# Stacking the high and low parts of the experts' results on the partitions of one product, in a two-layer kernel

## The reference, cut to what matters

```
expert = (g_idx * M_PER_GROUP + e_idx).reshape(-1)        # 2 of 32 experts per token
xs  = xt[tok_sorted]                                      # tokens, by expert
hid = silu(ragged_dot(xs, w_gate, sizes)) * ragged_dot(xs, w_up, sizes)   # 1024 -> 512
ys  = ragged_dot(hid, w_down, sizes) * weight             # 512 -> 1024
return segment_sum(ys, tok_sorted, num_segments=n_tok)    # back to the 512 tokens
```

## Time and profile before

| | |
|---|---|
| median of 3 runs | 2735.05 us (2734.01 to 2735.18) |
| profiled execution | 2735.55 us, its span in the trace 2733.7 us, 1.85 us around it |
| mean granted TensorE clock | 0.982 |
| PE busy | 2618.6 us (96%) |
| PEld / DVE / ACT / POOL busy | 1859.7 / 1461.6 / 749.7 / 114.4 us |
| bytes | 559.82 MB, mean 205 GB/s |
| the two expert stages, by the first and last start of their lines | about 226 to 730 and 1010 to 1515 us |

### The profile page before, as it was taken

One profiled execution on the slowest core, in us unless ns is written; L12 is line 12 of the kernel. 1 busy time (PEld: TensorE's weight loads), 2 busy tenths in 40 slices (PEclk: granted clock), 3 DMA queues, 4 the chain that ended last, 5 costly groups with the idle time before them and its releaser, 6 DMA issues. The chain is left out here.

```text
span 2733.7 us, 39425 instructions
## 1 busy us (share of the span) xinstructions
PE 2618.6 (96%) x15526; PEld 1859.7 (68%) x15526; DVE 1461.6 (53%) x2028; ACT 749.7 (27%) x1205; POOL 114.4 (4%) x238
## 2 busy tenths in 40 slices
PE   8997999999799979999999699999999999999999
PEld 7674555555476665555555577888888877888887
DVE  4755444444654554444444676656552666556632
ACT  3530000000145510000000343543332454433331
POOL 0000000000000000000000000000000010000000
PEclk9998999999899989999999899999999999999999
DMA  6249999999322089999997132223332312223331
GB/s 171 82 169 373 388 409 408 411 407 401 116 77 93 37 309 388 405 405 403 408 405 299 53 106 77 93 77 102 99 123 93 101 62 93 78 93 99 102 123 54
DMA packets 168109, 559.82 MB, mean 205 GB/s; under 512 B 17394, under 2 KB 100914, under 8 KB 118322
## 3 DMA queue, kind: packets, MB, share of 16 engines
q1 hardware_dynamic: 162546, 549.68, 53.4%
q0 software_dynamic: 5440, 8.40, 1.0%
HBM read 561.17 MB, written 6.29 MB: 208 GB/s over the span
## 5 line engine op out<-in xcount | busy, mean ns | idle before, releaser
L1401 DVE TENSOR_TENSOR resid<-resid,ps 128x1024 f32<-128x1024 f32 x252 | 306.8, 1218 | 237.7 <-PE ps L1321 237.7
L229 PE MATMUL ps<-l_h_hi,l_w_hi 128*128 128x512 f32 x896 | 352.9, 394 | 0.0
L230 PE MATMUL ps<-l_h_lo,l_w_hi 128*128 128x512 f32 x896 | 348.8, 389 | 0.0
L231 PE MATMUL ps<-l_h_hi,l_w_lo 128*128 128x512 f32 x896 | 348.7, 389 | 0.0
L1308 PE MATMUL ps<-first_weights,moe_xsT 128*64 128x256 f32 x2688 | 326.2, 384 | 0.0
L2885 DVE TENSOR_TENSOR l_w_lo<-l_raw,l_w_hi 128x2048 fp32r<-128x2048 f32 x76 | 174.0, 2292 | 270.6 <-ACT l_w_hi L2630 270.3
L1308 PEld LDWEIGHTS ps<-first_weights,moe_xsT 128*64 128x64 f32 x2688 | 191.5, 137 | 133.0 <-issue 67.4
L1373 ACT ACTIVATE moe_ys_hi<-ps 128x512 fp32r<-128x512 f32 x64 | 38.2, 597 | 687.3 <-PE ps L1347 687.3
L2630 ACT ACTIVATE l_w_hi<-l_raw 128x2048 fp32r<-128x2048 f32 x76 | 145.6, 1918 | 180.6 <-PE ps L231 161.1
L229 PEld LDWEIGHTS ps<-l_h_hi,l_w_hi 128*128 128x128 f32 x896 | 168.2, 188 | 37.6 <-issue 2.9
L230 PEld LDWEIGHTS ps<-l_h_lo,l_w_hi 128*128 128x128 f32 x896 | 168.3, 188 | 35.4 <-issue 1.4
(11 more groups left out here) (611 smaller groups left out, 4621.8 us busy)
## 6 DMA issues: line engine op xcount, KB each, us to landing
first_weights<-in_moe_w_up SPq DMA_DIRECT2D x84, 1024.0 KB, 11.5
first_weights<-in_moe_w_down SPq DMA_DIRECT2D x84, 1024.0 KB, 10.4
first_weights<-in_moe_w_gate SPq DMA_DIRECT2D x84, 1024.0 KB, 11.2
first_ring<-in_moe_w_up SPq DMA_DIRECT2D x44, 1024.0 KB, 11.7
first_ring<-in_moe_w_down SPq DMA_DIRECT2D x44, 1024.0 KB, 10.7
l_raw<-in_ffn_up SPq DMA_DIRECT2D x44, 1024.0 KB, 5.1
first_ring<-in_moe_w_gate SPq DMA_DIRECT2D x40, 1024.0 KB, 10.9
l_raw<-in_w_in SPq DMA_DIRECT2D x22, 1024.0 KB, 5.2
```

Source lines behind the costliest of these rows:

```text
L229: pe.matmul(out, stationary[0], moving[0], start=first, stop=False)
L230: pe.matmul(out, stationary[0], moving[1], start=False, stop=False)
L231: return pe.matmul(out, stationary[1], moving[0], start=False, stop=last)
L1401: dve.tensor_tensor(row, row, sums(t), ALU.add).then_inc(added, 1)
```

## The change

Four things change together, with the semaphores that go with them.

1. `ys_hi` and `ys_lo` become one tile `ys` [128, 2, 512]. For half h the 64 result rows stand twice on the partitions: high parts on the rows where the result lies, low parts on the other 64. One 128-row product per half with the same `sel` (whose 128 rows hold the slots twice) adds both. ACT and DVE write `ys` in two instructions each, one for each half of the partitions.
2. A row is gathered as two half rows: 128 indices, 128 rows of 2 KB, first halves on partitions 0-63, second halves on 64-127. `lay` makes the indices (twice the token, plus 0 or 1) for all 128 rows at once.
3. `turn_rows` transposes in pairs, one piece from each partition half, into two banks (`turned`); gate, up and the turned rows change places in PSUM.
4. The semaphores `sel_made` and `ys_low` become one, `parts_made`, with three counts per block; the wait for `ys_low` before the down products and one wait for `hid_kept` are gone; a wait for `silued` stands before `turn_rows`.

```diff
-            ins.then_inc(self.listed, 1)
+        ins.then_inc(self.listed, 1)
...
         dve.wait_ge(x.listed, 1)
-        dve.tensor_copy(x.near[0:SLOTS, :], k.ps[0:SLOTS, 3, 0:COLS]).then_inc(x.near_kept, 1)
-        dve.wait_ge(x.near_kept, 1)
-        dve.scalar_tensor_tensor(r.take[0:SLOTS, :], k.ps[0:SLOTS, 3, COLS:2 * COLS], float(NO_ROW), x.near[0:SLOTS, :], ALU.add, ALU.add).then_inc(x.done, 1)
+        link(dve.tensor_scalar(x.near[:, :], k.ps[:, 3, 0:COLS], float(NO_ROW), None, ALU.add))
+        link(dve.tensor_tensor(r.token, k.ps[:, 3, COLS:2 * COLS], x.near[:, :], ALU.add))
+        dve.tensor_scalar(r.take[:, :], r.token, 2.0, k.cst[:, C_HALF:C_HALF + 1], ALU.mult, ALU.add).then_inc(x.done, 1)
...
-    row_of_tile = xs[:, :].rearrange("s (c p j) -> s c j p", c=2, j=4)
+    row_of_tile = xs[:, :].rearrange("s (p j) -> s j p", j=4)
-    TURN, UP_BANK, DOWN, GATE = 0, 1, 2, 3
-    gate_out = lambda rows: k.ps[rows, GATE, 0:256]
+    TURN, GATE, DOWN, UP_BANK = 0, 1, 2, 3
+    gate_out = lambda rows: k.ps[rows, GATE, 256:512]
+    turned = k.ps[:, TURN:GATE + 1, 0:256]
...
-                pool.indirect_dma_start(out=xs[:, :], out_offset=None, in_=r.x_dram,
+                pool.indirect_dma_start(out=xs[:, :], out_offset=None, in_=r.half_rows,
                                         in_offset=bass.IndirectOffsetOnAxis(ap=take[:, 0:1], axis=0),
-                                        bounds_check=SEQ - 1, oob_is_err=False).then_inc(rows_in, 16)
+                                        bounds_check=2 * SEQ - 1, oob_is_err=False).then_inc(rows_in, 16)
...
-                wait_then_tick(pool, sel_made, b + 1, tick_pool)
+                wait_then_tick(pool, parts_made, 3 * b + 1, tick_pool)
...
             def turn_rows():
-                for j in range(ND):
-                    ins = pe.transpose(k.ps[:, TURN, j * SLOTS:(j + 1) * SLOTS], row_of_tile[:, j // 4, j % 4, :], k.cst[0:SLOTS, C_ID:C_ID + SLOTS])
+                for i in range(4):
+                    for c in range(2):
+                        rows_ = slice(64 * c, 64 * c + 64)
+                        ins = pe.transpose(turned[:, c, i * SLOTS:(i + 1) * SLOTS], row_of_tile[rows_, i, :], k.cst[rows_, C_ID + 64 * c:C_ID + 64 * c + 64])
...
                 if t == 0:
-                    wait_then_tick(pe, sel_made, b + 2, tick_pe)
-                    wait_then_tick(pe, ys_low, b + 2, tick_pe)
+                    wait_then_tick(pe, parts_made, 3 * b + 4, tick_pe)
...
-                for part in (ys_hi, ys_lo):
-                    for h in range(2):
-                        rows_ = slice(64 * h, 64 * h + 64)
-                        ins = pe.matmul(sums(t)[:, h, :], sel[rows_, t * P:(t + 1) * P], part[rows_, :], start=part is ys_hi, stop=part is ys_lo)
+                for h in range(2):
+                    ins = pe.matmul(sums(t)[:, h, :], sel[:, t * P:(t + 1) * P], ys[:, h, :], start=True, stop=True)
...
                 wait_then_tick(pe, xsT_kept, b + 1, tick_pe)
-
-                wait_then_tick(pe, hid_kept, b + 1, tick_pe)
...
                 wait_then_tick(pe, rows_in, b * 16 + 32, tick_pe)
+                wait_then_tick(pe, silued, b + 1, tick_pe)
                 turn_rows()
-                wait_then_tick(pe, hid_kept, b + 2, tick_pe)
+                wait_then_tick(pe, hid_kept, b + 1, tick_pe)
...
                 wait_then_tick(pe, hidT_kept, b + 1, tick_pe)
-                wait_then_tick(pe, ys_low, b + 1, tick_pe)
...
-                act.activation(ys_hi[:, :], k.ps[:, DOWN, :], ACT.Copy).then_inc(ys_kept, 1)
+                for h in range(2):
+                    rows_ = slice(64 * h, 64 * h + 64)
+                    act.activation(ys[rows_, h, :], k.ps[rows_, DOWN, :], ACT.Copy).then_inc(ys_kept, 1)
...
-                dve.tensor_scalar(sel[:, :], iota[:, :], slot[:, 1, :], None, ALU.is_equal).then_inc(sel_made, 1)
-                dve.wait_ge(ys_kept, b + 1)
-                dve.tensor_tensor(ys_lo[:, :], k.ps[:, DOWN, :], ys_hi[:, :].bitcast(F32), ALU.subtract).then_inc(ys_low, 1)
+                dve.tensor_scalar(sel[:, :], iota[:, :], slot[:, 1, :], None, ALU.is_equal).then_inc(parts_made, 1)
+                for h in range(2):
+                    high, low = slice(64 * h, 64 * h + 64), slice(64 - 64 * h, P - 64 * h)
+                    dve.wait_ge(ys_kept, 2 * b + h + 1)
+                    dve.tensor_tensor(ys[low, h, :], k.ps[high, DOWN, :], ys[high, h, :].bitcast(F32), ALU.subtract).then_inc(parts_made, 1)
```

More of the change, by code:

```diff
@@ L67 @@
 C_TOK = C_ISLOT + P
-C_MASKA = C_TOK + NT
+C_HALF = C_TOK + NT
+C_MASKA = C_HALF + 1
 C_MASKS = C_MASKA + 2 * P
@@ L107, in constants @@
     c[:, C_TOK:C_TOK + NT] = i[:, None] + P * np.arange(NT)
+    c[:, C_HALF] = i // SLOTS
     c[:, C_MASKA:C_MASKA + P] = np.where(i[None, :] > i[:, None], 0.0, NEG)
@@ L267, in __init__ @@
         self.le = plan.put("le", le_kb, [1, MORE_COLS, EXPERTS])
-        self.xs = plan.put("xs", xs_kb, [SLOTS, D])
-        self.ys_lo = plan.put("ys_lo", le_kb, [P, 512], F32R)
+        self.xs = plan.put("xs", xs_kb, [P, D // 2])
+        self.ys = plan.put("ys", le_kb - 2, [P, 2, 512], F32R)
         self.sel, self.iota = plan.put("sel", first_kb, [P, SEQ], F32R), plan.put("iota", first_kb + 2, [P, SEQ])
@@ L283, in __init__ @@
         (self.w_in, self.x_out, self.turned, taken_first, taken_second, self.made, self.shifted, self.ratioed, self.expd, self.chosen, self.ranked, self.laid,
-         self.listed, self.done, self.emptied, self.near_kept) = (st.sem(n) for n in (
-            "rw_in", "x_out", "rows_turned", "rows_taken_first", "rows_taken_second", "logits", "gshifted", "ratioed", "gexpd", "chosen", "ranked", "laid", "listed", "done", "emptied", "near_kept"))
+         self.listed, self.done, self.emptied) = (st.sem(n) for n in (
+            "rw_in", "x_out", "rows_turned", "rows_taken_first", "rows_taken_second", "logits", "gshifted", "ratioed", "gexpd", "chosen", "ranked", "laid", "listed", "done", "emptied"))
         self.taken = (taken_first, taken_second)
@@ L426, in lay @@
         ins.then_inc(x.laid, 1)
[L427 to L430, removed]
+        dve.wait_ge(x.listed, 2)
         link(dve.tensor_copy(x.near[:, :], k.ps[:, 7, 0:COLS]))
@@ L442, in first_rows @@
         pool.wait_ge(self.done, 1)
-        pool.indirect_dma_start(out=self.xs[:, :], out_offset=None, in_=r.x_dram,
-                                in_offset=bass.IndirectOffsetOnAxis(ap=r.take[0:SLOTS, 0:1], axis=0),
-                                bounds_check=SEQ - 1, oob_is_err=False).then_inc(r.rows_in, 16)
+        pool.indirect_dma_start(out=self.xs[:, :], out_offset=None, in_=r.half_rows,
+                                in_offset=bass.IndirectOffsetOnAxis(ap=r.take[:, 0:1], axis=0),
+                                bounds_check=2 * SEQ - 1, oob_is_err=False).then_inc(r.rows_in, 16)
     def list_experts(self, k, dve, link, r, listed):
@@ L1140, in __init__ @@
         self.x_dram = nc.dram_tensor(f"{name}_x", (SEQ, D), F32, kind="Internal").ap()
+        self.half_rows = self.x_dram.rearrange("s (h d) -> (s h) d", h=2)
 class ExpertWeights:
@@ L1205, in experts @@
     silu, hid, hidT = st.sb("silu", [P, 256]), st.sb("hid", [P, 256]), st.sb("hidT", [P, 2, P])
-    take, slot = st.sb("take", [SLOTS, 1], I32), st.sb("slot", [P, 2, 1])
-    ys_hi, ys_lo, sel, iota = st.sb("ys_hi", [P, 512], F32R), rt.ys_lo, rt.sel, rt.iota
-    (take_set, slot_set, rows_turned, xsT_kept, silued, hid_kept, hid_turned, hidT_kept, ys_kept, ys_low, sel_made, combined, added, tick_sp, tick_pool, tick_pe, chain,
+    take, slot = st.sb("take", [P, 1], I32), st.sb("slot", [P, 2, 1])
+    ys, sel, iota = rt.ys, rt.sel, rt.iota
+    (take_set, slot_set, rows_turned, xsT_kept, silued, hid_kept, hid_turned, hidT_kept, ys_kept, parts_made, combined, added, tick_sp, tick_pool, tick_pe, chain,
      expert_set, grown, first_hi) = (st.sem(n) for n in (
-         "take_set", "slot_set", "rows_turned", "xsT_kept", "silued", "hid_kept", "hid_turned", "hidT_kept", "ys_kept", "ys_low", "sel_made", "combined", "added",
+         "take_set", "slot_set", "rows_turned", "xsT_kept", "silued", "hid_kept", "hid_turned", "hidT_kept", "ys_kept", "parts_made", "combined", "added",
          "tick_sp", "tick_pool", "tick_pe", "chain", "expert_set", "grown", "first_hi"))
     rows_in = r.rows_in
-    row_of_tile = xs[:, :].rearrange("s (c p j) -> s c j p", c=2, j=4)
+    row_of_tile = xs[:, :].rearrange("s (p j) -> s j p", j=4)
     hid_of_tile = hid[:, :].rearrange("s (p j) -> s j p", j=2)
@@ L1254, in gather @@
             def gather(b):
-                pool.tensor_copy(take[:, :], r.take[0:SLOTS, bass.ds(b, 1)]).then_inc(take_set, 1)
+                pool.tensor_copy(take[:, :], r.take[:, bass.ds(b, 1)]).then_inc(take_set, 1)
                 wait_then_tick(pool, take_set, b, tick_pool)
-                pool.indirect_dma_start(out=xs[:, :], out_offset=None, in_=r.x_dram,
```

(9 more changed lines are left out.)

3 lines of the change are left out of this document (1 added, 2 removed).

## The result

The changed kernel took 2746.09 us (median of 5 runs, 2742.57 to 2750.44) against 2734.09 us (5 runs, 2733.82 to 2735.18) of the kernel before on the same chip: a ratio of 1.0044 [1.0031, 1.0057], 12.0 us slower. The forecast was 2744.3. The profiled execution of after is the longest of its five (2750.44 us, span 2748.6).

What follows compares the result with a forecast made beforehand. PE was taken to set the pace, with DMA keeping up. Terms 38.4 - 21.1 - 9.6 + 0 + 1.5 = +9.2 us gave 2744.3 us on the median's scale, range 2727 to 2767.

Steps and rivals of the forecast that it cites:

- A: Chain before combine t=0: ACT and DVE in 64-row halves end 0.60 us later per block, +38.4 us (34 to 44).
- B, turn in pairs: `turn_rows`: transposes in pairs let hidden transposes start 0.33 us sooner per block, until `hid` limits: -21.1 us.
- B, one wait less: Between `hidT`'s end and down's load: dropping the `ys_low` wait saves 0.15 us per block, -9.6 us.
- C: Combine: two 128-row products take as long as two pairs of 64 rows, shape change remains: 0, 6 us each way.
- start of a stage, gather: Layer starts: longer `lay` and first gather, about +2 us in layer 1, -0.6 in layer 0; gathers in loop cost nothing.
- rival 1: Combine's way in and out: shape change costs nothing once all products use 128 rows; -52, 2692 us; chance 0.08.
- Rival 2: Turn: the paired transposes take turns, so the -21.1 us gain falls away; 2765 us; chance 0.10.
- Rival 3: Terms nearly cancel: DVE's second half near 0.53 and a slightly cheaper combine; 2734 up to 2740 us; chance 0.20.
- Rival 4: Gather comes late, its 7.0 us doubled to 14.0: 25 to 56 us more, 2770 to 2800; chance 0.04.
- Rival 5: ACT and DVE halves overlap so well that t=0 is late by under 0.2 us; 2719 us or less; chance 0.06.

Runs made afterwards that it cites:

- halves_pairs: Changed kernel with ACT and DVE halves kept, but each combine again four products of 64 rows in pairs: 2748.84 us, ratio 1.0051.
- pairs_again: Changed kernel with whole ACT and DVE instructions and four 64-row products per combine again; half rows, paired turns and fewer waits stay: 2702.73 us.
- fewer_waits: Kernel before without the wait for `ys_low` ahead of down and the one for `hid_kept` at a block's start: 2725.91 us, ratio 0.9971.
- extra_wait: Changed kernel with one more, long-met wait before the down products: 2758.79 us, ratio 1.0084.
- late_pairs: `pairs_again` with its combines one place later, the last two behind the hidden transposes: 2664.61 us, ratio 0.9742 to the kernel before.
- late_stack: Changed kernel with its combines one place later, the last two behind the hidden transposes: 2655.84 us, ratio 0.9711 to the kernel before.
- turn_serial: Changed kernel with the eight turn transposes queued four for one row half, then four for the other: 2749.06 us, ratio 1.0047.
- one_wait: Changed kernel with DVE waiting for both of ACT's halves ahead of its first, none between its two subtractions: 2789.38 us, ratio 1.02.

## Why the prediction was right

The mechanism and the sign were as put on record, and the time, 2746.09, lies 1.8 us above the forecast. That it is so close is in part luck: A alone came out 7.7 us above its size in the sum, and the other terms together some 5 below theirs. The terms:

| step | predicted, us | measured, us | by |
|---|---|---|---|
| A, halves | +38.4 (34 to 44) | +46.1 | `halves_pairs` less `pairs_again` |
| B, turn in pairs | -21.1 | -23.2 | `pairs_again` less `fewer_waits` |
| B, one wait less | -9.6 | -8.5 | `fewer_waits` less before |
| C, one product | 0 (-6 to 6) | -2.8 | after less `halves_pairs`, within both intervals |
| start of a stage, gather | +1.5 | not resolved | within the line of the turn |
| sum | +9.2 | +11.6 | |

The four differences form one chain from the kernel before to after, so their sum comes to the 12.0 by itself, but for the 0.3 us between two medians of the kernel before; it is no check of the terms. What checks them is where in a block each difference lies, as given with the runs.

*A* is the term that was mis-sized, and it lay above its upper end. Halves of 591 and 688 ns are as said; the overlap of 0.09 between DVE's halves, taken from two adds, is not there. They start 0.72 apart, not 0.60, so the chain grew by 0.71 a block (PEld idle 1.16, not 1.05). The end of the range that stood for no overlap had 0.69; the distance between starts that these instructions show is 0.03 more.

*B, the turn.* The load of the hidden transposes came 0.77 after the turn, as forecast, and the limit named was the right one: `hid` ends at 444.01 + 0.48 = 444.49 and PE loads 0.12 later. *The waits.* `hidT` to down: 0.27, forecast 0.28. `extra_wait` shows that one wait more also costs, though 0.25 there.

*C.* Near zero in the time, for the reason given: two products of 128 rows take as long as two pairs of 64, and each combine between pieces still changes shape (0.67 us). Of the combines between pieces t=0's alone is shorter, by 0.03 (medians over blocks). Of rival 1 the premise failed, since 128x64 to 128x128 is a change too; the one place without a change, t=3, was covered, as the prediction said of it. The Trainium skill, TensorEngine Tiling (Array Packing), Key Properties, says that changing the tiling mode drains the array; the 0.18 us between `late_pairs` and `late_stack` agree with it.

*The other rivals.* Rival 2 fell with the 0.70 us of the turn and its products that start two at a time. Rival 3's small A did not come: A was larger. Rival 4 was a doubled landing; it is 6.4 us with 128 half rows, where it was 7.0, and layer 1's first gather lands after 6.1 us (issued at 1014.28, landed at 1020.39) instead of 6.9, so the +2 us for it did not show. (The 2.0 us that the prediction puts down to an empty queue are the last two gathers of each layer, for blocks that don't exist and so without a valid index; they say little of a gather with rows.) Rival 5 fell with the 1.41 us of DVE's halves. The start of a stage can't be read from these traces: the time between the two layers' expert loops lies between 296.8 and 305.1 us over the kernels, most of which have the same code there.

What the prediction didn't see: A was a cost of place, not of work. It counted PE's one piece as cover that had been used up, which was right, but with the next piece 0.94 us of slack is left, for an edit of a few lines.

## What to carry to other kernels

Before a chain on ACT and DVE is made longer, read the idle time of the consumer that follows it: here 0.06 us of lateness meant that every added nanosecond arrived at the end, and the same halves one piece of work later cost nothing. Splitting these instructions by partitions doubled their time, 0.60 to 1.21 us on ACT and 0.69 to 1.41 on DVE, so it pays only where the chain has slack. The stacked product was worth something at one place, where the product ahead of it has the same shape and, with the combines moved, nothing else is awaited (`late_stack`).

## What the runs showed of the hardware that was not expected

- Eight transposes on two row halves took 0.70 us queued alternately and 0.70 us queued four and four; in both orders they start two at a time, a pair every 0.12 us (after, `turn_serial`).
- Two DVE subtractions of 64x512 from PSUM start 0.72 us apart at 0.69 us each, with or without a wait between them (`one_wait`), while two adds of 128x1024 took 2.35 us at 1.218 each.
- From 128*128 to 64*128 PE's next weights came 0.18 us later than from 128*128 to 128*128 (`late_pairs`, `late_stack`).
- A wait that had long been met cost PE 0.15 us ahead of down, where nothing covers it (`fewer_waits`), and 0.25 with a value that needed a register operation (`extra_wait`).
